# A hybrid decoder kernel: the matrix-memory update taken by pairs of chunks, and the cached values in two halves of TensorE's columns

## The chip, the cores and the metric

The kernel is one program on one core of a Trainium2 chip. The metric is the device time of one execution in microseconds, and for a kernel the median of its runs.

A core has engines that run beside each other and wait for one another through semaphores. The profile calls them PE (TensorE's matmuls), PEld (its weight loads), DVE (VectorE), ACT (ScalarE), POOL (GpSimd) and SP (which here only issues DMAs). A matmul on full fp32 operands has two records in the trace, one for each pass; a transpose, and a product of the large matrices in the kernel's fp32r halves, has one.

## What is computed

A trunk of two layers runs for one prompt of 1024 tokens and eight sample tokens. Each layer has a projection `w_in`, sliding-window attention for eight heads (group A), a matrix memory for eight other heads (group B), an output projection `w_out`, a gated feed-forward and a per-layer embedding. The change concerns group B on the prompt, and the attention of the sample tokens over cached keys and values:

```python
def mlstm_chunk(carry, inp):          # one chunk of 128 tokens, the carry goes to the next
    ...
    sc = jnp.einsum('bhtk,bhsk->bhts', q, k) * dw
    num = iw[..., None] * jnp.einsum('bhvk,bhtk->bhtv', C, q) + jnp.einsum('bhts,bhsv->bhtv', sc, v)
    den = iw * jnp.einsum('bhk,bhtk->bht', n, q) + jnp.sum(sc, axis=-1)
    h = num / jnp.maximum(jnp.abs(den), jnp.exp(-m_t))[..., None]
    ...
    C_new = cw[..., None, None] * C + jnp.einsum('bhs,bhsv,bhsk->bhvk', ws, v, k)
    n_new = cw[..., None] * n + jnp.einsum('bhs,bhsk->bhk', ws, k)
```

```python
def dilated_gather_stats(q, k_all, v_all, window, dilation, buf_len):   # sample tokens, three patterns
    ...
    s = jnp.einsum('bthd,btjhd->bthj', q.astype(jnp.float32), kg) * (HEAD_DIM ** -0.5)
    ...
    o = jnp.einsum('bthj,btjhd->bthd', e, vg) / l[..., None]
```

## The kernel before

The program is written out by hand: every engine has its own list in Python, in the order in which the engine runs it, and waits name a semaphore and a count (`at(...)` adds the layer's offset). Nothing reorders it. A large product is split into a rounded half `hi` and a rest `lo`, so each product of a weight tile is three matmuls (`three`, L923 to L925). GpSimd makes the rest of every weight block (`split`, L868) after ScalarE has rounded it (`round_block`, L1483).

Group B's stage goes over four head pairs, `q` = 0 to 3, and in each over eight chunks `c` of 128 tokens. While TensorE works on pair `q` it also computes the projection of pair `q + 1` in small pieces (`next_products`), five or six steps of three matmuls before each chunk (`ahead_b`). Pair 3 has no next one: there the pieces are the cached values of the sample tokens (`sample_values`, L1038), 24 matmuls of 64 output rows by 512 columns. The stage takes from about 380 to 640 us in layer 0 and from about 1966 to 2221 us in layer 1; the output projection follows it.

For a chunk, TensorE runs, in this order:

- `kq` (L1216): keys by queries for the two heads, each on 64 of the array's 128 rows, into PSUM banks 0 and 1. It waits until the chunk before has been read out.
- the update U (L1271): weighted keys by values, 128x130.
- the chunk's own output (L1290): two matmuls of 65 columns.
- the output from the memory C (L1295), 130 columns, which needs the memory after the chunk before (`c_upd`).

VectorE's part is `prepare(c)`: weighted keys (L2327) and masked scores (L2331); and `finish(c)`: it waits for the update and both outputs, writes the new memory in place (L2341), and makes the output rows (L2345 to L2349), which set `n_read`. Behind them it has the sample tokens' keys: `sample_keys` (L2366, L2367), 24 pieces in pairs 0 and 1, one or two behind each chunk, from two buffers in `kvb`. SP loads piece i when piece i-2 has been used, and every third piece also needs a row of queries. Pair 0 also has a reciprocal square root there.

At the end of a head pair TensorE turns the memory (L1310), which needs the last `finish`; then it goes on with `next_products(0, 6)` and `turn_qk` of the next pair.

In pair 3, VectorE also updates the sample tokens' memory, behind the chunks given: `memory_gates` (1), `memory_keys` (2, waits for `state_C`), `memory_output` (3), `y_sums`, `memory_gated` (waits for `mo_in`, L779's DMA) and `memory_update` (5), then `y_root` and `normalise(0..2)` (6). ScalarE scales and rounds two blocks of `w_out` meanwhile, between the squares of the outputs (`output_squares`, L1689), and GpSimd multiplies the gates in (`gated`, L887), then splits the two blocks one behind the other. After the chunks, TensorE turns the rows of three token tiles (`turn_y`, L1199), ScalarE and VectorE write their halves (L1786, L2438), and the output projection starts; behind its first eighth stands `turn_y(3)`, which needs `y_root(2, ...)` (L2253) and `normalise(3)` (L2265, L2266).

## Time and profile before

| | |
|---|---|
| median of 3 runs | 3222.62 us (3222.48 to 3223.53) |
| span of the profiled execution | 3219.3 us |
| PE busy in it | 3117.2 us, 97% |
| DVE busy | 1854.2 us, 58% |
| mean granted TensorE clock | 0.990 |
| matmul records | 19459 |

The span goes from the first to the last instruction; the median of the runs is 3.3 us above it, which is what lies around the instructions. "Granted clock" is 1.00 at TensorE's upper level, 2.4 GHz, and 0.50 at 1.2 GHz. In rows with a bracket, the bracket is how long the engine had been idle before the row and what it had waited for. The end of a matmul is modelled: a record of 128 columns lasts some 0.27 us, but the next can start 0.11 us after it; so the cost of matmuls is read from the distance of their starts.

### The profile page before, as it was taken

The page shows a single profiled execution, that of the slowest core. Times are in us where ns is not written, and L with a number is a line of the kernel's source. Part 1 is how long each engine was busy: PE and PEld are TensorE (multiplying, and loading weights), DVE is VectorE, ACT ScalarE, POOL GpSimd, SP SyncE. Part 2 cuts the span into 40 slices and gives each one's busy share as a digit, 9 for nine tenths or more (in the row PEclk, how much of TensorE's full clock was granted, in tenths as well). Part 3 has the DMA queues.
Part 4 walks back from the last instruction along what each step waited for, and adds up shares of the span by engine and source line. Part 5 has one row for each costly group of instructions (what it writes and reads, how often), then busy time and mean ns, then how long its engine had stood idle before and what let it go on. Part 6 is the DMA issues. An engine that isn't in the chain of part 4 may idle for free.

```text
span 3219.3 us, 50875 instructions
## 1 busy us (share of the span) xinstructions
PE 3117.2 (97%) x19459; PEld 2847.0 (88%) x19459; DVE 1854.2 (58%) x4369; ACT 1027.8 (32%) x2117; POOL 901.3 (28%) x2061
## 2 busy tenths in 40 slices
PE   7999999899999999999999999998999999999999
PEld 7887777599999999999987777766999999999998
DVE  5676465655555555557467755647555555555663
ACT  4444344533111111115344433455321111111251
POOL 3111122505322324223322210333232333223231
PEclk8999999999999999999999999999999999999999
DMA  5211234512111111110221111336111121111111
GB/s 172 55 47 49 56 83 120 177 51 66 40 53 40 40 66 40 53 40 21 94 69 47 47 50 48 109 106 195 53 40 40 40 66 40 53 40 40 40 37 71
DMA packets 228570, 208.87 MB, mean 65 GB/s; under 512 B 36676, under 2 KB 207620, under 8 KB 226736
## 3 DMA queue, kind: packets, MB, share of 16 engines
q1 hardware_dynamic: 228328, 205.62, 21.1%
q8 instruction: 154, 2.52, 0.3%
q14 instruction: 88, 0.72, 0.1%
HBM read 173.96 MB, written 31.61 MB: 64 GB/s over the span
## 4 chain that ended last, share of the span: by engine, by line
PE 87%; DVE 8%; ACT 2%; issue 1%; POOL 1%; DMA 1%; SPq 0%; DVEq 0%; ACTq 0%
PE ps L923 25%; PE ps L925 24%; PE ps L924 24%; PE ps L1095 2%; PE ps L1066 2%; PE ps L1081 2%; POOL wlo L868 1%; PE ps L1038 1%; PE ps L1216 1%; PE ps L1290 1%; DVE lo L1943 1%; DVE att L2112 1%; DVE att L2101 1%; PE ps L1199 0%; PE ps L1031 0%
## 5 line engine op out<-in xcount | busy, mean ns | idle before, releaser
L868 POOL TENSOR_TENSOR wlo<-raw,whi 128x128 fp32r<-128x128 f32 (+3 forms) x1952 | 857.1, 478 | 1833.4 <-ACT whi L1483 1404.9
L923 PE MATMUL ps<-hi,wlo 128*128 128x344 f32 x2880 | 927.8, 322 | 10.0 <-POOL wlo L868 8.1
L925 PE MATMUL ps<-hi,whi 128*128 128x344 f32 x2880 | 922.3, 320 | 0.0
L924 PE MATMUL ps<-lo,whi 128*128 128x344 f32 x2880 | 921.6, 320 | 0.0
L923 PEld LDWEIGHTS ps<-hi,wlo 128*128 128x128 f32 x2880 | 544.4, 189 | 13.6 <-POOL wlo L868 8.6
L925 PEld LDWEIGHTS ps<-hi,whi 128*128 128x128 f32 x2880 | 543.5, 189 | 0.0
L924 PEld LDWEIGHTS ps<-lo,whi 128*128 128x128 f32 x2880 | 542.9, 188 | 0.6
L923 PE MATMUL ps<-whi,lo 128*128 128x512 f32 (+3 forms) x1056 | 413.4, 391 | 4.8 <-POOL wlo L868 4.3
L925 PE MATMUL ps<-whi,hi 128*128 128x512 f32 (+3 forms) x1056 | 390.3, 370 | 0.0
L924 PE MATMUL ps<-wlo,hi 128*128 128x512 f32 (+3 forms) x1056 | 388.7, 368 | 0.0
L2530 DVE TENSOR_TENSOR X<-X,ps 128x344 f32<-128x344 f32 x528 | 268.0, 511 | 184.7 <-PE ps L925 182.9
L1838 ACT ACTIVATE wb<-wb 128x344 f32<-128x344 f32 x132 | 64.9, 492 | 969.2 <-DVE wb L2517 969.2
L923 PE MATMUL ps<-yhi,wlo 128*128 128x344 f32 x1056 | 340.0, 322 | 0.7 <-DVE X L2530 0.7
L925 PE MATMUL ps<-yhi,whi 128*128 128x344 f32 x1056 | 338.3, 320 | 0.0
L924 PE MATMUL ps<-ylo,whi 128*128 128x344 f32 x1056 | 337.4, 319 | 0.0
L923 PEld LDWEIGHTS ps<-whi,lo 128*128 128x128 f32 (+1 forms) x1056 | 196.7, 186 | 67.1 <-issue 28.2
L925 PEld LDWEIGHTS ps<-whi,hi 128*128 128x128 f32 (+1 forms) x1056 | 196.7, 186 | 26.7
L2509 DVE TENSOR_TENSOR wa<-ps,rstd 128x344 f32<-128x344 f32 x132 | 68.2, 517 | 261.6 <-PE ps L925 261.2
L924 PEld LDWEIGHTS ps<-wlo,hi 128*128 128x128 f32 (+1 forms) x1056 | 197.6, 187 | 20.3
L1483 ACT ACTIVATE whi<-raw 128x2048 fp32r<-128x2048 f32 (+3 forms) x106 | 188.1, 1782 | 44.8 <-DMA raw<-in_w_down 33.7
L923 PEld LDWEIGHTS ps<-yhi,wlo 128*128 128x128 f32 x1056 | 198.7, 188 | 1.8 <-DVE X L2530 1.6
L924 PEld LDWEIGHTS ps<-ylo,whi 128*128 128x128 f32 x1056 | 198.3, 188 | 0.2
(325 smaller groups left out, 3873.6 us busy)
## 6 DMA issues: line engine op xcount, KB each, us to landing
raw<-in_w_up SPq DMA_DIRECT2D x44, 1024.0 KB, 5.1
raw<-in_w_in SPq DMA_DIRECT2D x112, 256.0 KB, 4.4
raw<-in_w_down SPq DMA_DIRECT2D x22, 1024.0 KB, 4.9
kvb<-in_cache_win_k SPq DMA_DIRECT2D x48, 256.0 KB, 3.3
cache<-in_cache_win_v SPq DMA_DIRECT2D x42, 256.0 KB, 3.7
X<-x_scratch SPq DMA_DIRECT2D x4, 2064.0 KB, 11.1
raw<-in_w_out SPq DMA_DIRECT2D x8, 1024.0 KB, 8.5
raw<-in_w_ple_gate SPq DMA_DIRECT2D x8, 1024.0 KB, 5.2
```

The source lines that it names most:

```text
L868: pool.tensor_tensor(out=wlo[:, s, r], in0=raw[:, s, r], in1=whi[:, s, r].bitcast(F32), op=ALU.subtract).then_inc(w_split, 1)
L923: nc.tensor.matmul(out, a_lo, b_hi, start=first, stop=False)
L924: nc.tensor.matmul(out, a_hi, b_lo, start=False, stop=False)
L925: return nc.tensor.matmul(out, a_hi, b_hi, start=False, stop=last)
L1038: nc.tensor.matmul(ps[0:HD, 6, :].rearrange("p (k n) -> p k n", k=4), weight_place(i), value_place(i), start=(i == ORDER[0]), stop=(i == O ...
L1066: mm = nc.tensor.matmul(ps[:, 2 * e + a // 4, 0:(b - a) * P].rearrange("p (t n) -> p t n", n=P), q3[r, qb, :], k3[r, a:b, :], start=True, ...
L1081: mm = nc.tensor.transpose(ps[:, 4 + half, (kb % 4) * P:(kb % 4 + 1) * P], att[:, a:a + P], ident[:, :])
L1095: mm = nc.tensor.matmul(ps[HD * e:HD * e + HD, 6, 0:P], zt[:, p % 2, kb, zc:zc + HD], att[:, a:a + P], start=(kb == 0), stop=(kb == qb))
L1483: do(nc.scalar.activation(whi[:, s, 0:used], raw[:, s, 0:used], ACT.Copy), w_hi, wait=False)
L1838: do(nc.scalar.activation(w, w, ACT.Gelu_apprx_tanh), gelu_done, wait=False)
L2509: do(v.tensor_tensor(out=w[:, 2:CH + 2], in0=ps[:, s % 3, 0:CH], in1=rstd[:, col(c)], op=ALU.mult), gate_read)
L2530: do(v.tensor_tensor(out=x, in0=x, in1=ps[:, 5 + (24 * i + j) % 3, 0:CH], op=ALU.add), dn_read, wait=False)
```

## The change

- **Keys by queries, four chunks together.** `kq` makes eight matmuls for four chunks, which fill banks 0 and 1; it runs twice for a head pair (before the first chunk, and in the second pair of chunks) and no longer eight times.
- **Chunks in pairs `j`.** The updates of two chunks stand together, and so do their four own-output matmuls. The outputs from the memory stay apart, with the second chunk's projection piece between them. VectorE's `prepare` and `outputs_b` take two chunks in one instruction each, where they can.
- **Two memory places.** An update reads one place and writes the other, so `states` need not wait for the chunk's own output from memory. `states`, `prepare` and `outputs_b` replace `prepare` and `finish`, and the sample keys of two chunks now stand behind one another.
- **The memory's turn** (`turn_memory`) stands behind `next_products(0, 6)` of the next pair.
- **Cached values.** Two of the 24 matmuls write to PSUM partitions 0 to 63 and 64 to 127; the two sums are added at the end (`sample_out`, `sample_sum`: one instruction more of 64x512, and a reduction over twice the elements).
- **The queue of SP in pair 3:** `state_C` is loaded ahead of the last five value strips.
- In pair 3, `memory_output` moves up behind the second pair of chunks, `memory_gated` stands behind the third, and `y_sums` and `memory_update` between the states and the outputs of the fourth.

```diff
-VALUES = (6, 9, 11, 13, 15, 17, 19, 20, 20)
+VALUES = (6, 10, 14, 18, 20)
@@ sample_values
-                    for i in ORDER[first:last]:
-                        pe.wait_ge(*at(v_in[value_group(i)], (128, 128, 48, 80)[value_group(i)]))
-                        nc.tensor.matmul(ps[0:HD, 6, :].rearrange("p (k n) -> p k n", k=4), weight_place(i), value_place(i),
-                                         start=(i == ORDER[0]), stop=(i == ORDER[-1])).then_inc(v_used, 1)
+                    for n in range(first, last, 2):
+                        for i in ORDER[n:n + 2]:
+                            pe.wait_ge(*at(v_in[value_group(i)], (128, 128, 48, 80)[value_group(i)]))
+                        for z, i in enumerate(ORDER[n:n + 2]):
+                            nc.tensor.matmul(ps[z * HD:(z + 1) * HD, 6, :].rearrange("p (k n) -> p k n", k=4), weight_place(i), value_place(i),
+                                             start=(n == 0), stop=(n + 2 == 3 * NB)).then_inc(v_used, 1)
@@ TensorE
+                def turn_memory(q):
+                    pe.wait_ge(*at(c_upd, 9 * (q + 1)))
+                    ...
-                    def kq(c):
-                        if c:
-                            pe.wait_ge(*at(sc_done, NT * q + c))
-                        for e in range(2):
+                    def kq(half):
+                        for x in range(4):
+                            c = 4 * half + x
+                            for e in range(2):
...
                         next_products(0, 6)
-                        pe.wait_ge(*at(c_upd, 9 * q))
+                        turn_memory(q - 1)
...
-                    for c in range(NT):
-                        ...
+                    for j in range(NT // 2):
+                        g, c = 4 * q + j, 2 * j
                         next_products(ahead_b(q, c), ahead_b(q, c + 1))
+                        ...
+                        pe.wait_ge(*at(sc_done, g + 1))
+                        if j == 1:
+                            kq(1)
+                        ...
+                        if q + 1 == PAIRS:
+                            sample_values(VALUES[j], VALUES[j + 1])
+                        for x in range(2):
+                            if x:
+                                next_products(ahead_b(q, c + 1), ahead_b(q, c + 2))
+                            pe.wait_ge(*at(c_upd, 9 * q + c + x + 1))
+                            nc.tensor.matmul(ps[:, 3 + j % 2, x * VW:(x + 1) * VW], att[:, 2 * SEQ + (c + x) * P:2 * SEQ + (c + x + 1) * P],
+                                             Cst2[:, 2 * (q % 2) + x, :], start=False, stop=(x == 1)).then_inc(n_ready, 1)
@@ VectorE
+                    def states(j):
+                        dve.wait_ge(*at(u_ready, 4 * q + j + 1))
+                        for x in range(2):
+                            c = 2 * j + x
+                            dve.wait_ge(*at(n_ready, NT * q + c))
+                            ...
-                    for c in range(NT):
+                    for j in range(NT // 2):
...
-                        finish(c)
+                        states(j)
+                        if last and j == 3:
+                            y_sums(0, 6)
+                            memory_update()
+                        if j + 1 < NT // 2:
+                            prepare(j + 1)
+                        outputs_b(j)
...
-                            for i in keys_of(q, c):
-                                sample_keys(i)
+                            for c in (2 * j, 2 * j + 1):
+                                for i in keys_of(q, c):
+                                    sample_keys(i)
...
-                        elif c == 3:
                             memory_output()
-                        elif c == 5:
-                            y_sums(0, 5)
+                        elif j == 2:
                             memory_gated()
-                            memory_update()
```

TensorE in head pair 3 of layer 0, from the turn of the memory. Before, with `kq` (L1216) at each chunk and three and two value strips (L1038) behind the first chunks:

```order
L1038 MATMUL ps<-cache,vectors 64x512 x4
L1216 MATMUL ps<-rstd,kT 128x128 x2
L1271 MATMUL ps<-zt,att 128x130
L1216 MATMUL ps<-rstd,kT 128x128 x2
L1290 MATMUL ps<-zt,att 128x65 x2
L1295 MATMUL ps<-Cst,att 128x130
L1038 MATMUL ps<-cache,vectors 64x512 x3
```

And now (`kq` is L1226, the update L1290, own outputs L1306, outputs from memory L1314, value strips L1042):

```order
L1042 MATMUL ps<-cache,vectors 64x512 x4
L1226 MATMUL ps<-rstd,kT 128x128 x8
L1290 MATMUL ps<-zt,att 128x130 x2
L1306 MATMUL ps<-zt,att 128x65 x4
L1042 MATMUL ps<-cache,vectors 64x512 x4
L1314 MATMUL ps<-Cst,att 128x130 x2
L1290 MATMUL ps<-zt,att 128x130 x2
L1226 MATMUL ps<-rstd,kT 128x128 x8
```

Eight `kq` matmuls stand where two stood, and the value strips have moved ahead of the outputs from memory.

TensorE at the end of head pair 0, before (L1310 is the turn of the memory, L923 to L925 are the next pair's projection):

```order
L932 MATMUL ps<-whi,thin 40x512
L1271 MATMUL ps<-zt,att 128x130
L1290 MATMUL ps<-zt,att 128x65 x2
L1295 MATMUL ps<-Cst,att 128x130
L1310 MATMUL ps<-ident,Cst 64x128 x2
L923 MATMUL ps<-whi,lo 128x512
```

And the turn now (L1211), 18 projection matmuls (L925 to L927) later:

```order
L925 MATMUL ps<-whi,lo 128x512
L926 MATMUL ps<-wlo,hi 128x512
L927 MATMUL ps<-whi,hi 128x512
L1211 MATMUL ps<-ident,Cst 64x128 x2
L1055 MATMUL ps<-ident,zt 128x128 x16
```

The turn stands between the last of these and the turn of the next pair's queries and keys (L1055).

VectorE in head pair 1, behind two chunks, before:

```order
L2341 SCALAR_TENSOR_TENSOR Cst<-Cst,cwb,ps 64x65 x2
L2345 SCALAR_TENSOR_TENSOR den<-ps,em 128x2
L2347 TENSOR_TENSOR den<-ps,den 128x2
L2348 RECIPROCAL den<-den 128x2
L2349 TENSOR_TENSOR yb<-ps,den 128x128
L2327 SCALAR_TENSOR_TENSOR att<-zt,att 128x128
L2331 SCALAR_TENSOR_TENSOR att<-ps,att 128x256
L2366 TENSOR_TENSOR kvb<-kvb 128x512
L2367 TENSOR_REDUCE att<-kvb 128x8
L2366 TENSOR_TENSOR kvb<-kvb 128x512
L2367 TENSOR_REDUCE att<-kvb 128x8
```

And now, for a pair of chunks (states L2351, prepare L2336 and L2340, outputs L2360 to L2364), with the first two of the four key pieces behind it:

```order
L2351 SCALAR_TENSOR_TENSOR Cst<-Cst,cwb,ps 64x65 x4
L2336 SCALAR_TENSOR_TENSOR att<-zt,att 128x128 x2
L2340 SCALAR_TENSOR_TENSOR att<-ps,att 128x2x256
L2360 SCALAR_TENSOR_TENSOR den<-ps,em 128x4
L2362 TENSOR_TENSOR den<-ps,den 128x4
L2363 RECIPROCAL den<-den 128x4
L2364 TENSOR_TENSOR yb<-ps,den 128x256
L2381 TENSOR_TENSOR kvb<-kvb 128x512
L2382 TENSOR_REDUCE att<-kvb 128x8
L2381 TENSOR_TENSOR kvb<-kvb 128x512
L2382 TENSOR_REDUCE att<-kvb 128x8
```

Two more key pieces follow without other work between them, then the next pair's states.

## Rows read from the trace of the kernel before

**Rows 1.** The page: busy time, and the chain that ended last

```profile
PE 3117.2 (97%) x19459; PEld 2847.0 (88%) x19459; DVE 1854.2 (58%) x4369; ACT 1027.8 (32%) x2117; POOL 901.3 (28%) x2061
PE 87%; DVE 8%; ACT 2%; issue 1%; POOL 1%; DMA 1%; SPq 0%; DVEq 0%; ACTq 0%
```

**Rows 2.** Windows, layer 0, in pairs 0 and 3: PE, PEld, DVE, ACT, POOL, clock, DMA

```profile
407.00:445.00 38.00, 38.00 (x208) 29.76 (x208) 29.16 (x90) 19.00 (x51) 16.52 (x34) 1.00 0.21 63
582.00:640.00 58.00, 48.97 (x205) 24.88 (x204) 42.98 (x125) 34.72 (x87) 24.54 (x57) 0.88 0.65 218
```

**Rows 3.** Timeline of PE, a chunk of head pair 1, and the next one's memory output

```profile
483.39 0.38 PE L1271 MATMUL ps<-zt,att 128*128 128x130 f32 x2
483.61 0.56 PE L1290 MATMUL ps<-zt,att 128*128 128x65 f32 x4
484.00 0.44 PE L1295 MATMUL ps<-Cst,att 128*128 128x130 f32 x2
484.37 0.49 PE L1216 MATMUL ps<-rstd,kT 64*128 64x128 f32 x4
484.79 0.50 PE L923 MATMUL ps<-whi,lo 128*128 128x512 f32 x1
485.13 0.40 PE L924 MATMUL ps<-wlo,hi 128*128 128x512 f32 x1
485.37 0.39 PE L925 MATMUL ps<-whi,hi 128*128 128x512 f32 x1
...
489.69 0.44 PE L1295 MATMUL ps<-Cst,att 128*128 128x130 f32 x2
```

**Rows 4.** Timeline of PE: matmuls that share the array, or don't

```profile
1960.89 1.97 PE L1095 MATMUL ps<-att,zt 128*64 128x128 f32 x32
...
588.02 3.65 PE L1038 MATMUL ps<-cache,vectors 128*64 128x512 f32 x8
```

**Rows 5.** Timeline of PE: the memory's turn at the ends of pairs 0 and 1

```profile
445.93 0.41 PE L1310 MATMUL ps<-ident,Cst 128*64 128x128 f32 x2 [0.92 <-DVE Cst L2341]
513.42 0.41 PE L1310 MATMUL ps<-ident,Cst 128*64 128x128 f32 x2 [2.47 <-DVE Cst L2341]
```

**Rows 6.** Timeline of DVE, a chunk of head pair 1

```profile
484.59 0.59 DVE L2341 SCALAR_TENSOR_TENSOR Cst<-Cst,cwb,ps 64x65 f32<-64x65 f32 x2 [0.75 <-PE ps L1295]
...
486.67 0.68 DVE L2366 TENSOR_TENSOR kvb<-kvb 128x512 f32<-128x512 f32 x1
...
488.11 0.69 DVE L2366 TENSOR_TENSOR kvb<-kvb 128x512 f32<-128x512 f32 x1
```

**Rows 7.** DMA issues of the keys: the page, then 455:457 (us to landing)

```profile
kvb<-in_cache_win_k SPq DMA_DIRECT2D x48, 256.0 KB, 3.3
...
kvb<-in_cache_win_k SPq DMA_DIRECT2D x2, 256.0 KB, 9.0
```

**Rows 8.** Timeline, pair 3 of layer 0: what DVE and PE wait for

```profile
610.25 2.29 DVE L2222 TENSOR_TENSOR vectors<-vectors,mz 128x2048 f32<-128x2048 f32 x1 [3.95 <-DMA vectors<-in_state_C]
612.92 0.80 PE L1271 MATMUL ps<-zt,att 128*128 128x130 f32 x2 [4.79 <-DVE att L2327]
```

**Rows 9.** Timeline before the turn of the fourth tile, layers 0 and 1

```profile
637.14 6.70 POOL L868 TENSOR_TENSOR wlo<-raw,whi 128x128 fp32r<-128x128 f32 x16
639.66 4.21 DVE L2253 SCALAR_TENSOR_TENSOR yt<-yrs 128x3 f32<-128x3 f32 x1
644.96 1.09 PE L1199 MATMUL ps<-ident,att 128*128 128x128 f32 x8 [1.11 <-DVE att L2266]
2219.22 6.69 POOL L868 TENSOR_TENSOR wlo<-raw,whi 128x128 fp32r<-128x128 f32 x16
2220.82 5.11 DVE L2253 SCALAR_TENSOR_TENSOR yt<-yrs 128x3 f32<-128x3 f32 x1
2227.03 1.09 PE L1199 MATMUL ps<-ident,att 128*128 128x128 f32 x8 [2.02 <-DVE att L2266]
```

**Rows 10.** Windows: granted clock after the wait at 513.4

```profile
514.00:518.00 4.00, 4.00 (x13) 3.16 (x12) 2.90 (x8) 1.50 (x5) 0.41 (x1) 0.60 0.09 11
```

More of the change, by code:

```diff
@@ L1284, in _ @@
                             sample_turn()
[L1285 removed]
+                        if j >= 2:
                             pe.wait_ge(*at(n_read, g - 1))
[L1287 to L1291 removed]
@@ new lines, in _ @@
+                        for x in range(2):
+                            if x:
[3 more added lines that the diff above has]
+                                             Cst2[:, 2 * (q % 2) + x, :], start=False, stop=(x == 1)).then_inc(n_ready, 1)
```

210 lines of the change are left out of this document (99 added, 111 removed).

## The prediction

> **What bounds the kernel now.** I read the page first. Its busy line has PE at 97% of the span, and the chain that ended last goes over PE for 87% and over DVE for 8% [rows 1]. So a change counts where it takes occupied time from TensorE, and where DVE holds TensorE up. I looked at the stage of the head pairs by windows. In pair 0 PE is busy for the whole 38.00 us, at full clock. In pair 3 it is busy for 48.97 of 58, at a clock of 0.88, with DVE busy for 42.98 [rows 2]: TensorE has too little left to do there, and follows DVE. So there are two kinds of stage. In pairs 0 to 2 each us of TensorE counts as long as DVE keeps up; in pair 3 TensorE's work is almost free, and DVE's order of work and the DMAs that it awaits decide. Next I took the timeline of PE for one chunk, to price its switches of form, then every row of PE with a wait in the stage, and for each wait DVE's timeline in the same stretch, to see what it had been doing. Last came the landings of the keys' DMAs.
>
> The sum is made against the profiled execution: its span of 3219.3 us, to which the median adds 3.3 us that lie around the instructions.
>
> **Keys by queries, 8 visits to 2.** The two passes of the output from memory start at 484.00, and the same width took 0.22 us between 483.39 and 483.61, so they are over at about 484.22. The products run at a distance of 0.23 (485.13 to 485.37, and so for all that follow). Without `kq` the second product would start near 484.45; it starts at 485.13 [rows 3]. The visit costs 0.68 us. Its four records of 128 columns, two beside each other, are two passes of about the width that took 0.11 each: 0.22 to 0.24 us of real streaming. So 0.44 us of each visit is going into the form with 64 rows and coming out of it; the weight load before it and the one behind it don't lie under a running matmul. The streaming stays, six visits of eight go: 6 x 0.44 = 2.6 us for each head pair. Pairs 0 to 2 of two layers are six: -15.8 us. If the second visit of a head pair or the new place of `kq` before the updates keeps part of it, less; the lowest I can see is half, -8. For pair 3 I count nothing, since DVE is late there anyway.
>
> The Trainium skill ("TensorEngine Tiling (Array Packing)", Key Properties) says that a change of the tiling mode drains TensorE. The trace agrees in kind, with 0.44 us a visit; the page gives no figure, and the updates and own outputs, whose grouping changes no form, should by it give nothing. They are counted at nothing in the sum too.
>
> **The turn of the memory, behind 18 products.** Today TensorE reaches it at once and waits 0.92 us at the end of pair 0 and 2.47 at the end of pair 1 [rows 5]; layer 1 repeats both within 0.12 us. Now the turn stands 18 x 0.23 = 4.1 us later, which covers both: 2 x (0.92 + 2.47) = -6.8 us. At the end of pair 2 no products stand between, and the wait stays. After the wait of 2.47 us the clock is 0.60 for the next 4 us [rows 10], some 1.6 us lost. I give this no gain, since the next term makes stalls of nearly that length. The cover is gone if DVE is more than 4 us late at the end of pair 1; the next step says how late.
>
> **Keys, now four behind one another.** In pair 1 a key piece takes DVE 1.44 us (486.67 to 488.11), and everything else of a chunk 2.08 (484.59 to 486.67) [rows 6]. Two chunks come to 4.16, some 3.6 with the outputs' four small instructions once for both; four pieces are 5.8. Together that is 9.4 us, while TensorE needs twice 5.69 less two visits of 0.65, or about 10.1 us (484.00 to 489.69) [rows 3]. By busy time DVE fits. But there are two buffers. The third piece's load starts when the first has been read, 1.4 us into the burst, and lands after 3.3 us [rows 7]: at 4.7 instead of 2.9. The fourth's buffer is free at 2.9, and it lands at 6.2, just as the third is done. The burst is then 7.6 us long instead of 5.8, and DVE's cycle 3.6 + 7.6 = 11.2 us. Today one or two pieces stand behind a chunk, and the other work hides their loads. The next outputs from memory need `states`, which stand behind the burst. TensorE's cycles in pair 1 are near 10.1, 11.1 (with `kq(1)` in it) and 8.3 (the last, which has only the next update and one piece of projection before it needs the memory). It waits 1.1 + 0.1 + 2.9 us, of which the 0.75 us that DVE idles today [rows 6] is to be taken once: about 3.2 us in each layer, +6.4. In pair 0, with one piece a chunk, the cycle fits; I add 0.3 a layer, +0.6. The bounds are nothing (the loads land between instructions) and +10 (each lands in 4.2 us).
>
> **Pair 3.** The value strips now share the array. A group of 8 without a partner takes 3.65 us, 0.46 each with 512 columns; 32 records of 128 columns that do share it take 1.97, which is 0.06 each, so 0.24 for 512 [rows 4]. So TensorE's time for the strips about halves, some 5 us a layer. But it waits there, so this alone counts nothing. What matters is DVE's order. Today DVE waits 3.95 us for `state_C`, and TensorE in turn 4.79 for the weighted keys that stand behind it [rows 8]. `state_C` goes ahead of five strips and lands earlier, so that DVE is up to 3.95 us ahead from there on. The next late transfer is `mo_in`, which doesn't move ahead: `memory_gated` awaits it behind the third pair of chunks, and behind it stand the last two chunks. I estimate 3.5 us earlier at the start of the output projection, in either layer. The extra instruction of `sample_out` (0.7 us, as a key piece's first in [rows 6]) and the wider sum (about 1 us) lie behind the start, where DVE has time.
>
> Then comes the place that decides. `y_root`'s three-column instruction L2253, usually 0.2 us, took 4.21 us in layer 0 and 5.11 in layer 1, and it ended with GpSimd's run of 16 splits, at 643.8 and 2225.9; TensorE waited 1.11 and 2.02 us for what stands behind it [rows 9]. GpSimd's splits come behind its gates, and the last gate behind ScalarE's last squares, which in turn wait for the last outputs. I find that these end hardly 0.5 us earlier than now, as `memory_update` now stands ahead of them. The projection starts 3.5 us sooner, but its fourth tile's turn comes at the old time. Gain 0.6 us in both layers together; the wait of TensorE grows to nearly 5 us, and the clock is then low as in [rows 10], 1.6 us once more than today. +1.0 us.
>
> The Trainium skill ("SBUF — State Buffer", SBUF: two separate sides) has a lock for a port pair that VectorE, with two SBUF inputs, and GpSimd share, for one instruction. By that rule DVE should wait for one split, 0.42 us (6.70 over 16), and be free; the row shows ten of them. The measurement decides for the case that I forecast; the rule speaks for the second one below.
>
> **Sum.** -15.8 - 6.8 + 6.4 + 0.6 + 1.0 = -14.6: a span of 3204.7, and 3208.0 us.
>
> **Rivals.** *A, the forecast, 0.45.* L2253's successor is held to the end of the splits again.
>
> *B, not held, 0.27.* It now has two elements a row for three, and may come at another place of GpSimd's run. Then both layers keep their 3.5 us and lose the waits of 1.11 and 2.02 us: 10.1 less 1.6 for a clock that falls anyway, -8.5 where A has +1.0. That is 3198.5 us. For it speaks that in the rest of the trace DVE is seldom held; against it, two of two.
>
> *C, dearer bursts or cheaper visits, 0.18.* The bursts at their bound (+10 for +7.0), or half of `kq`'s saving kept back (+7.9): 3211 to 3216.
>
> *D, the change gives nothing in its main part, 0.06.* If four pairs of `kq` matmuls still cost 0.68 each, the saving of 15.8 is gone, and 3208 + 15.8 = 3224 us. Against it speaks the run of 32 that share the array at 0.06 us each [rows 4].
>
> *E, slower, 0.04.* The keys' loads: two of them took 9.0 us to landing with weights on the way [rows 7]. Should the burst's loads take that, the third piece starts at 10.4 us and the fourth at 11.9, the burst ends at 13.3, and the cycle is 16.9: 5.7 us more than I have, in three cycles of both layers, +34. 3242 us. It decides from loads of some 5.8 us on, where the cycle is 2.5 us longer, which is 15 in six cycles. Against it: the median of 48 is 3.3.
>
> **How the numbers follow.** A at 3208.0 with half of the bursts' bounds either way is 3204 to 3211; B 3195 to 3201; C to 3216. The range 3196 to 3216 holds A, most of B and C, and leaves out D, E and the lower edge of B. A difference from no change shows from about 0.2%, 6.4 us. Faster is below 3216.2: A, B and nearly all of C, 0.89. D and the rest of C are 0.07; E with a larger D 0.04.
>
> **What the changed profile would show.** `kq` in 16 visits, 48 fewer than the 64 of today, and after each other output from memory products at the regular distance, without the 0.68 us. No wait at the memory's turn in pairs 0 and 1. In pair 1 DVE waits for the keys' DMA in the third piece of each burst, TensorE for `states` at the first output from memory, together 3 us a layer. `memory_keys` without a wait of 3.95 us, `memory_gated` with one for `mo_in`. The start of the output projection 3.5 us sooner against the end of pair 2; and the length of the three-column instruction's successor, 4 us or 0.2, which tells A from B. I would be wrong if the second `kq` of a head pair waited for scores not yet read, if `states`, which now wait for two updates and two outputs, came late by themselves in pairs 0 and 2, or if the turn of the memory waited in its new place.

## The result: slower

The changed kernel takes 3234.4 us (median; 3230.1 to 3237.6), the kernel before 3222.6: a ratio of 1.0037, 95% interval 1.0025 to 1.0049. I had forecast 3208.0, faster, in a range of 3196 to 3216, and had given slower 0.04. Run once more, later, it had 3238.8 beside 3223.8, 1.0046 (1.0031 to 1.0061). Below, kernels are compared by their ratio to the kernel before on the same chip as well as by medians, since the kernel before itself had 3220.9 to 3223.8 on the chips used.

The page of the changed kernel, which answers to [rows 1]:

```profile
span 3230.0 us, 50619 instructions
...
PE 3097.3 (96%) x19459; PEld 2843.7 (88%) x19459; DVE 1840.2 (57%) x4211; ACT 1027.8 (32%) x2117; POOL 893.5 (28%) x2061
...
PE 83%; DVE 9%; ACT 2%; issue 2%; DMA 1%; POOL 1%; SPq 1%; DVEq 0%; ACTq 0%
```

TensorE has 20 us less work, as meant, and yet the span is 10.7 us longer. In the chain, SP's queue, which had 0% before, has 1%, and PE has 83% for 87%. Where the time went shows when the span is cut at TensorE's landmarks (starts of the turn of queries and keys, of the first `kq` of a head pair, and of the eighth tile's turn; us in layer 0, layer 1). "Two edits", "pool" and "split first" are kernels of the experiments below.

| stretch | before | changed | two edits | three edits, pool | and split first |
|---|---|---|---|---|---|
| pair 0: first `kq` to pair 1's turn | 43.4, 43.3 | 43.4, 43.1 | 45.0, 45.0 | 41.3, 41.4 | 41.2, 41.3 |
| pair 1: the same | 52.1, 50.6 | 51.1, 51.8 | 52.2, 51.8 | 49.6, 48.8 | 47.3, 47.2 |
| pair 2's turn to its first `kq` | 17.0, 16.9 | 25.6, 25.3 | 17.3, 17.3 | 17.3, 18.1 | 17.3, 17.3 |
| pair 2 | 45.7, 45.7 | 41.9, 41.9 | 41.9, 41.9 | 41.9, 41.9 | 41.9, 41.9 |
| pair 3's first `kq` to the eighth tile's turn | 72.0, 71.0 | 71.2, 72.5 | 73.2, 70.4 | 67.0, 66.4 | 67.1, 66.9 |

One stretch holds more than the whole loss: behind pair 1, 8.6 and 8.4 us. I had not looked at it. Pair 2, the only one without sample keys, gains 3.8 us. Pairs 0 and 1, where most of the saving was to be, gain next to nothing. A stretch is read from one profile, and it can differ by 3 us between two profiles of one kernel: the second profile of the changed kernel has 46.1 and 44.6 us in pair 0 and 52.2 in both layers in pair 1, but 25.6 and 25.5 behind it. The timeline of PE in the changed kernel, layer 0: four rows with waits in pairs 0 to 2, and the memory's turn (L1211):

```profile
445.23 0.49 PE L1314 MATMUL ps<-Cst,att 128*128 128x130 f32 x2 [3.19 <-DVE Cst L2351]
...
449.72 0.38 PE L1211 MATMUL ps<-ident,Cst 128*64 128x128 f32 x2
...
501.75 0.75 PE L1314 MATMUL ps<-Cst,att 128*128 128x130 f32 x2 [2.03 <-DVE Cst L2351]
...
513.15 0.49 PE L1314 MATMUL ps<-Cst,att 128*128 128x130 f32 x2 [1.30 <-DVE Cst L2351]
...
535.99 0.80 PE L925 MATMUL ps<-whi,lo 128*128 128x512 f32 x1 [6.55 <-ACT zt L1563]
```

The turn of the memory (L1211) no longer waits, against 0.92 us in [rows 5]: as forecast. But the last output from memory (L1314) ahead of it waits 3.19, and the projection of the next pair 6.55 us; in layer 1 the waits are 2.79, 1.19, 2.96 and 6.28.

**The wait of 6.55 us, followed back.** TensorE waits for ScalarE (L1563), which frees a PSUM bank. Its timeline in the changed kernel:

```profile
519.50 0.60 ACT L1602 ACTIVATE rstd<-ps 128x512 f32<-128x512 f32 x1 [0.21 <-PE ps L1055]
534.95 0.47 ACT L1559 ACTIVATE zt<-ps,rcol 128x256 f32<-128x256 f32 x1 [14.85 <-DMA z_scratch<-zt]
```

The timeline of SP's queue in the changed kernel:

```profile
511.15 9.41 SPq L669 DMA_DIRECT2D kvb<-in_cache_win_k  x3
520.93 1.15 SPq L741 DMA_DIRECT2D mg<-g_scratch  x2
...
525.96 1.21 SPq L572 DMA_DIRECT2D raw<-in_w_out  x2
527.22 1.25 SPq L638 DMA_DIRECT2D z_scratch<-zt  x2
```

And in the kernel before, in the same place:

```profile
505.84 5.55 SPq L668 DMA_DIRECT2D kvb<-in_cache_win_k  x3
511.76 1.15 SPq L740 DMA_DIRECT2D mg<-g_scratch  x2
...
518.38 1.47 SPq L637 DMA_DIRECT2D z_scratch<-zt  x2
```

ScalarE waits until the sample tokens' rows of pair 2 have been copied out of the place that it is to write. That copy (L638, before L637) stands in SP's queue behind the key loads of pair 1, and a key load waits until a buffer has been used. The last of them went out at 511.4 (505.84 + 5.55) and now at 520.6 (511.15 + 9.41); eight small loads and two weight blocks follow, so the copy is issued at 527.2, not 518.4. VectorE's timeline of the kernel before, from the key whose buffer the last load takes:

```profile
510.35 0.69 DVE L2367 TENSOR_REDUCE att<-kvb 128x8 f32<-128x512 f32 x1
...
515.16 0.22 DVE L2357 COPY cT<-ps 64x64 f32<-64x64 f32 x1
...
515.66 0.69 DVE L2366 TENSOR_TENSOR kvb<-kvb 128x512 f32<-128x512 f32 x1
```

VectorE's timeline of the changed kernel says why that key is used so late:

```profile
511.78 0.69 DVE L2382 TENSOR_REDUCE att<-kvb 128x8 f32<-128x512 f32 x1
512.50 1.24 DVE L2351 SCALAR_TENSOR_TENSOR Cst<-Cst,cwb,ps 64x65 f32<-64x65 f32 x4
...
518.29 0.22 DVE L2372 COPY cT<-ps 64x64 f32<-64x64 f32 x1 [2.64 <-PE ps L1211]
...
519.52 0.69 DVE L2382 TENSOR_REDUCE att<-kvb 128x8 f32<-128x512 f32 x1
520.24 0.69 DVE L2381 TENSOR_TENSOR kvb<-kvb 128x512 f32<-128x512 f32 x1
...
522.97 0.69 DVE L2381 TENSOR_TENSOR kvb<-kvb 128x512 f32<-128x512 f32 x1 [1.32 <-DMA kvb<-in_cache_win_k]
```

Three keys stand behind the copy of the turned memory (L2372) where one stood before. The first of them, whose buffer the last load takes, is done at 520.2 (519.52 + 0.69) and was done at 511.0 (510.35 + 0.69): 9.2 us later, as is the load. Of these, 2.64 us are VectorE's wait for the turn, which has been put 18 products later. The rest comes from the pairing: that key now stands behind the states and outputs of the last two chunks, and stood ahead of the last chunk's.

### The profile page after: what moved, and what is told of

It reads as the page before. It is cut to its first block, busy times and chain, and to the rows that moved or that the text cites. A ratio compares the mean times of both kernels' runs of the same rounds, so it can differ in the third digit from the quotient of the medians.

```text
span 3230.0 us, 50619 instructions
## 1 busy us (share of the span) xinstructions
PE 3097.3 (96%) x19459; PEld 2843.7 (88%) x19459; DVE 1840.2 (57%) x4211; ACT 1027.8 (32%) x2117; POOL 893.5 (28%) x2061
## 4 chain that ended last, share of the span: by engine, by line
PE 83%; DVE 9%; ACT 2%; issue 2%; DMA 1%; POOL 1%; SPq 1%; DVEq 0%; ACTq 0%
PE ps L925 24%; PE ps L927 24%; PE ps L926 24%; PE ps L1099 2%; PE ps L1070 2%; PE ps L1085 2%; POOL wlo L870 1%; DMA kvb<-in_cache_win_k 1%; DVE kvb L2381 1%; DVE lo L1952 1%; PE ps L1306 1%; PE ps L1203 1%; DVE att L2121 1%; DVE att L2382 1%; DVE att L2110 1%
## 5 line engine op out<-in xcount | busy, mean ns | idle before, releaser
L925 PE MATMUL ps<-hi,wlo 128*128 128x344 f32 x2880 | 928.3, 322 | 12.0 <-POOL wlo L870 8.1
L927 PE MATMUL ps<-hi,whi 128*128 128x344 f32 x2880 | 922.5, 320 | 0.0
L925 PEld LDWEIGHTS ps<-hi,wlo 128*128 128x128 f32 x2880 | 544.7, 189 | 15.6 <-POOL wlo L870 8.6
L927 PEld LDWEIGHTS ps<-hi,whi 128*128 128x128 f32 x2880 | 543.8, 189 | 0.0
L925 PE MATMUL ps<-whi,lo 128*128 128x512 f32 (+3 forms) x1056 | 415.1, 393 | 15.4 <-ACT zt L1563 13.2
L927 PE MATMUL ps<-whi,hi 128*128 128x512 f32 (+3 forms) x1056 | 391.3, 371 | 0.0
L925 PE MATMUL ps<-yhi,wlo 128*128 128x344 f32 x1056 | 339.9, 322 | 0.7 <-DVE X L2546 0.7
L927 PE MATMUL ps<-yhi,whi 128*128 128x344 f32 x1056 | 338.3, 320 | 0.0
L925 PEld LDWEIGHTS ps<-whi,lo 128*128 128x128 f32 (+1 forms) x1056 | 198.2, 188 | 74.8 <-issue 27.0
L927 PEld LDWEIGHTS ps<-whi,hi 128*128 128x128 f32 (+1 forms) x1056 | 197.6, 187 | 27.0
L925 PEld LDWEIGHTS ps<-yhi,wlo 128*128 128x128 f32 x1056 | 198.7, 188 | 1.5 <-DVE X L2546 1.3
## 6 DMA issues: line engine op xcount, KB each, us to landing
X<-x_scratch SPq DMA_DIRECT2D x4, 2064.0 KB, 10.7
```

What stands on the lines that cost most here:

```text
L925: nc.tensor.matmul(out, a_lo, b_hi, start=first, stop=False)
L927: return nc.tensor.matmul(out, a_hi, b_hi, start=False, stop=last)
```

## The experiments

**Small loads last.** In SP's queue of pair 1 the small loads go behind the copies.

```diff
-                    if h2 == 1:
-                        ...
                     if p < 2 * PAIRS - 2:
                         load_pair(p + 3)
                     store_pair(p + 1)
                     sp.wait_ge(*at(o_exp, h2 + 1))
                     sp.dma_start(Zd[6, :, h2 * P:h2 * P + P], zt[0:NB, p % 2, NT, OG:ZW]).then_inc(z_stored[p % 2], 16)
+                    if h2 == 1:
+                        ...
```

> The changed kernel, but in SP's queue of head pair 1 the twelve small loads for the memory of the sample tokens (gates, m, n) stand behind the copy of the third pair's sample rows and not ahead of it. Queue theory: TensorE's new wait of 6.55 and 6.28 us at the start of pair 2 is the end of a chain: the last key piece is used late, SP's queue can't pass its load, and the copy that ScalarE awaits stands behind it and behind 5.0 us of small issues. Then the copy goes 5.0 us sooner, the wait falls to about 1.5 us in each layer and the clock stays up: some 12 to 14 us less than the changed kernel's 3234.4, so 3221 to 3223. Rival, key bursts alone: the 8.5 us lost there come from DVE being late behind the keys; the order of small loads does nothing, 3232 to 3236, wait as before.

(There are eight of these loads, not twelve.) 3229.8 us, 1.0024 (1.0014 to 1.0035). TensorE's waits are 2.00 and 1.31 us, the stretch takes 19.5 and 18.8. So the small loads have a part in the wait, as said, but the median is only 5 us lower, where the stretch gave up 12.6: in this profile pair 3 takes 74.0 and 74.7 us to the eighth tile's turn.

**Keys before the turned memory.** In pair 1 `store_turned` goes behind the last keys.

```diff
                             if j == 3:
                                 tile_sum(p + 1)
-                                store_turned()
+                                if q != 1:
+                                    store_turned()
                             ...
                                     sample_keys(i)
+                            if j == 3 and q == 1:
+                                store_turned()
```

> The changed kernel, but at the end of head pair 1 VectorE takes the last four key pieces ahead of the copy of the turned memory, for which it waited 2.6 us in the new place. Queue theory: the last key load is released about 3.4 us sooner, so the copy lands 3.4 us sooner and TensorE waits about 3.1 us and not 6.5: 3227 to 3229. If the moved turn has no part in it: no change, 3232 to 3236. A cost of its own: TensorE may wait for the turned memory's bank, up to 1 us.

3228.7 us, 1.0017 (1.0006 to 1.0028); the waits are 2.70 and 2.18 us. The time is as expected and the waits are a little shorter. So the keys' place behind the turn's copy has a part.

**The turn at the end of its pair**, the other way round.

```diff
-                        turn_memory(q - 1)
...
                                              Cst2[:, 2 * (q % 2) + x, :], start=False, stop=(x == 1)).then_inc(n_ready, 1)
+                    turn_memory(q)
```

> The changed kernel, but the memory's turn stands at the end of its head pair, as before. The prediction's term said that moving it behind 18 products saves 6.8 us: undone, 3234.4 + 7 = 3241. Queue theory: states now stand ahead of the outputs, so the turn waits under 1 us there, and the copy of the turned memory, and with it the last keys and the rows' copy, come 3.5 us sooner: 3228 to 3231.

3233.5 us, 1.0040 (1.0025 to 1.0055): neither theory's time. The waits behind pair 1 fall to 2.84 and 1.23 us and that stretch to 21.9 and 18.8, as the queue theory has it, but the median is only 0.9 us under the first runs of the changed kernel, and the interval holds the ratios of both of its measurements, 1.0037 and 1.0046. It is not 7 us higher either. In its timeline of PE the turn at the end of pair 1 does not wait:

```profile
515.73 0.80 PE L1313 MATMUL ps<-Cst,att 128*128 128x130 f32 x2 [2.96 <-DVE Cst L2350]
516.37 0.64 PE L1211 MATMUL ps<-ident,Cst 128*64 128x128 f32 x2
```

So the turn had nothing to gain from the move, since `states` now come ahead of the outputs. Where the 10 us of the stretch went is open: its profile has them spread over pairs 0, 1 and 3, by amounts that also differ between profiles of one kernel.

**Both order edits**, beside the changed kernel itself on one chip.

> The changed kernel once more, unchanged, beside the next one. It had 3234.4 us (3230.1 to 3237.6), ratio 1.0037. Expected again 1.003 to 1.0045; it shows how far kernels with idle stretches of TensorE differ from one chip and profile to the next.

> The changed kernel with the small loads behind the rows' copy and the last keys ahead of the turned memory's copy, and the bursts of keys as they are. Queue theory: the wait of 6.55 and 6.28 us at the start of pair 2 is gone in both layers and the stretch from the turn of pair 2's queries to its first key-query products takes 17 us instead of 25.5: up to 17 us, of which pair 3 may take back 2 to 5 (as with the small loads last): 12 to 15 us less than the changed kernel beside it, so 3220, about the kernel before. If the queue is not the cause of most of it: 5 to 8 us.

The changed kernel again: 3238.8 us, 1.0046 (1.0031 to 1.0061). With both edits: 3221.6 us, 0.9994 (0.9985 to 1.0004), 17.2 us less, more than the 12 to 15 expected and as much as the stretch behind pair 1 gives up (8.3 and 8.2 us: 25.6 and 25.5 to 17.3). TensorE has no wait there:

```profile
521.60:538.90 17.30, 17.30 (x90) 12.56 (x89) 6.86 (x14) 8.83 (x29) 0.00 (x0) 1.00 0.60 181
```

In the changed kernel the same window (columns as in [rows 2]) is:

```profile
518.00:543.60 25.60, 19.05 (x91) 13.48 (x89) 8.92 (x16) 9.81 (x32) 0.00 (x0) 0.87 0.50 140
```

19.05 us of work instead of 17.3 at a clock of 0.87, and 6.55 of wait. This settles the cause of the loss: the copy that comes late in SP's queue. What is left, no gain, has to come from pairs 0 and 1.

**Keys around the outputs.** Two of a burst's keys go ahead of `outputs_b`, which waits for TensorE anyway.

```diff
+                        early = [i for c in (2 * j, 2 * j + 1) for i in keys_of(q, c)]
+                        early = early[:2] if len(early) > 2 and j < 3 else []
+                        for i in early:
+                            sample_keys(i)
                         outputs_b(j)
...
-                                    sample_keys(i)
+                                    if i not in early:
+                                        sample_keys(i)
```

> The changed kernel, but where more than two key pieces follow in one burst, the first two stand ahead of the outputs (j below 3), so that DVE works on them while it would wait for TensorE's second output from memory, and the third piece's load has the outputs' 1 us and that wait to land. Burst theory: TensorE's waits for the states inside pairs 0 and 1 (2.79 to 3.19, 1.2 to 2.0, 1.3 to 3.0 us, 13.5 us in the two layers) shrink to a third, and with the queue wait untouched the time falls by 7 to 9 us: 3225 to 3227. Rival: these waits come from two pairs of chunks' states being taken together, not from the bursts: under 2 us.

3223.7 us, 1.0001 (0.9992 to 1.0011): 10.7 us less than the changed kernel, more than the 7 to 9 expected. Inside pairs 0 and 1 six waits of 13.5 us became one of 0.98 and three for the projection's next piece of 1.38, 1.14 and 1.57, and pair 1 takes 47.2 and 47.4 us. The queue's wait is still 6.59 and 6.31. This shows that the waits come from the bursts; they cost 13.5 us where I had 7.0. In the changed kernel a burst of pair 1 looks like this:

```profile
479.48 0.69 DVE L2381 TENSOR_TENSOR kvb<-kvb 128x512 f32<-128x512 f32 x1
...
480.92 0.69 DVE L2381 TENSOR_TENSOR kvb<-kvb 128x512 f32<-128x512 f32 x1
...
483.57 0.69 DVE L2381 TENSOR_TENSOR kvb<-kvb 128x512 f32<-128x512 f32 x1 [1.24 <-DMA kvb<-in_cache_win_k]
...
486.60 0.69 DVE L2381 TENSOR_TENSOR kvb<-kvb 128x512 f32<-128x512 f32 x1 [1.62 <-DMA kvb<-in_cache_win_k]
...
488.05 1.23 DVE L2351 SCALAR_TENSOR_TENSOR Cst<-Cst,cwb,ps 64x65 f32<-64x65 f32 x4
```

8.6 us from the first key to the states, where I had 7.6; the other bursts of pair 1 have DMA waits of 3.41 and 1.40 us. And in pair 0 a burst of three at 436.5 waits 3.48 us for its third, a burst that I had priced at 0.3.

**The kernel before, with `kq` in fours** in pairs 0 and 1 only.

```diff
+                        if q < 2 and c % 4:
+                            return
+                        for x in range(4 if q < 2 else 1):
                             for e in range(2):
-                                mm = nc.tensor.matmul(ps[:, e, 0:P], kT[r, c * P:(c + 1) * P], ...
+                                mm = nc.tensor.matmul(ps[:, e, x * P:(x + 1) * P], kT[r, (c + x) * P:(c + x + 1) * P], ...
```

> The kernel before, with only one part of the change: in head pairs 0 and 1 the key-query products of four chunks are made together (two visits for eight), everything else where it was; pairs 2 and 3 as before. Drain theory (0.44 us saved a visit, six visits in each of four head pairs of the two layers): -10.6 us, 3212. Rival: the drain is paid again elsewhere, or DVE, which takes 42% longer to get a free chunk, holds TensorE at the end of each pair, so the wait at the memory's turn grows and half of it is lost: 3217. If nothing is saved: 3222.6.

3223.1 us, 1.0006 (0.9995 to 1.0017): nothing. (The 42% in the expectation had no basis and stands for nothing.) Its timeline of PE in pair 1:

```profile
474.13 0.38 PE L1274 MATMUL ps<-zt,att 128*128 128x130 f32 x2
...
479.17 0.38 PE L1274 MATMUL ps<-zt,att 128*128 128x130 f32 x2
...
489.28 0.38 PE L1274 MATMUL ps<-zt,att 128*128 128x130 f32 x2
...
490.27 1.16 PE L1219 MATMUL ps<-rstd,kT 64*128 64x128 f32 x16
...
495.66 0.39 PE L1274 MATMUL ps<-zt,att 128*128 128x130 f32 x2
...
509.80 0.49 PE L1274 MATMUL ps<-zt,att 128*128 128x130 f32 x2 [0.63 <-DVE att L2330]
...
514.53 0.64 PE L1313 MATMUL ps<-ident,Cst 128*64 128x128 f32 x2 [3.46 <-DVE Cst L2345]
```

A chunk without a visit takes 5.04 us, one with the visit of four 6.38, against 5.69 each in [rows 3]: 4 x 5.69 - 3 x 5.04 - 6.38 = 1.26 us for four chunks, 2.5 a head pair. My 2.6 was right. But the pair as a whole is no shorter: the turn's wait grew from 2.47 to 3.46 us, with 0.63 more ahead of it, and in pair 0 three waits of 0.37, 0.80 and 1.02 stand for the one of 0.92. VectorE, which in pair 1 of layer 0 waited 6.8 us for outputs from memory (L1295) before, waits 3.5 us for them here, and 2.0 for keys. So it has little slack in pairs 0 and 1: time taken from TensorE there comes back as waits for VectorE, and those at the pairs' ends were the sign of it. The granted clock has a part too, 0.94 in pair 1 in both layers for 0.97 and 1.00.

**The kernel before, with the values in halves.**

```diff
-VALUES = (6, 9, 11, 13, 15, 17, 19, 20, 20)
+VALUES = (6, 8, 10, 12, 14, 16, 18, 20, 20)
...
-                                         start=(i == ORDER[0]), stop=(i == ORDER[-1])).then_inc(v_used, 1)
+                                             start=(n == 0), stop=(n + 2 == 3 * NB)).then_inc(v_used, 1)
```

> The kernel before, with only the values part: two of the 24 matmuls share the array and write to 64 partitions each, six ahead, then two behind each chunk; one more instruction of 64x512 and a reduction twice as wide. Theory of the prediction: 5 us of TensorE's work less in pair 3 of each layer is worth nothing there, as DVE decides; within 1 us of 3222.6. Rival: less work means more idle time and a lower granted clock in pair 3 (0.87 and 0.91 before, 0.78 in the changed kernel), which lengthens what follows: 1 to 4 us slower.

3220.9 us, 0.9999 (0.9989 to 1.0008): no difference, as predicted. The clock in pair 3 fell (0.68 from its first `kq` to the first tile's turn in layer 0, for 0.87), and the time does not show it; TensorE waits there in both kernels.

**Three edits.** Small loads last, keys before the turned memory, keys around the outputs.

> The changed kernel with three edits of order together: the small loads behind the sample rows' copy, the last keys of pair 1 ahead of the turned memory's copy, and two of each burst's keys ahead of the outputs. Queue theory: each alone left a part of the wait at the start of pair 2 (1.3 to 2.0 us with the small loads last, 2.2 to 2.7 with the keys first); together it is gone, and that stretch takes 17.0 us again instead of 25.5; the two layers give 17 us, of the kernel with the keys around the outputs at 3223.7: 3205 to 3209. Rival, from the traces of the last kernels: pair 3 takes what is gained before it (38.6 us to the first turned tile instead of 36.1 in layer 0), since a transfer there lands at a fixed time: 3213 to 3217.

3212.3 us, 0.9972 (0.9962 to 0.9982). Between the two theories; the stretch behind pair 1 is 17.4 and 17.3 us, but pair 1 takes 49.5 and 49.7, as TensorE now waits 2.23 and 2.55 us for GpSimd's splits at its end.

**Three edits, and GpSimd's last 16 splits wait for the root.**

```diff
                         gated(q, NT - 1, NT)
+                        pool.wait_ge(*at(yr_two, 1))
                         split(B + n + 1)
```

> The kernel with three edits, and GpSimd's last run of 16 splits waits until VectorE has the root for the last two tiles. Hold theory: the root's first instruction took 5.99 and 6.27 us only because it met the run of splits; now it takes 0.2, the fourth tile's turn comes 5 us sooner in each layer, TensorE's waits of 2.9 and 3.2 us go, with some of the low clock behind them: 5 to 8 us less than the three edits alone. Rival: the instruction waits for something else that comes at that time (an activation, a square), then it keeps its 6 us; or the splits, now 1.5 us later, hold TensorE in the projection: no gain.

3202.5 us, 0.9937 (0.9921 to 0.9954): 9.8 us less than without it, more than expected. From the first tile's turn to the eighth it takes 30.7 and 30.9 us, for 35.0 and 35.4. This is the place where A and B parted. In the changed kernel the root's first instruction for two tiles was held longer than in [rows 9], again to the end of GpSimd's run (646.7):

```profile
640.78 5.99 DVE L2262 SCALAR_TENSOR_TENSOR yt<-yrs 128x2 f32<-128x2 f32 x1
...
640.05 6.69 POOL L870 TENSOR_TENSOR wlo<-raw,whi 128x128 fp32r<-128x128 f32 x16
```

and with the splits waiting for it:

```profile
631.53 0.15 DVE L2263 SCALAR_TENSOR_TENSOR yt<-yrs 128x2 f32<-128x2 f32 x1
...
632.16 7.08 POOL L870 TENSOR_TENSOR wlo<-raw,whi 128x128 fp32r<-128x128 f32 x16 [1.65 <-DVE yrs L2265]
```

**The same wait alone**, in the changed kernel and in the kernel before.

> The changed kernel with the wait of GpSimd's last 16 splits for the root alone. With the three edits it was worth 9.75 us. The hold was 5.99 and 6.27 us here: 8 to 10 us less than the changed kernel, 3224 to 3227. If the gain of 9.75 needed the other edits (which move the stage against the transfers), under 4 us.

> The kernel before, with only the wait of GpSimd's last 16 splits for the root. Its instruction L2253 was held 4.21 and 5.11 us and TensorE waited 1.11 and 2.02 us behind it, so the kernel before has the cost too, but less of it: 3 to 5 us, with the low clock behind the waits, 3217 to 3219. If before and changed kernel gain alike (9 us), the hold has no part in the change being slower.

Changed kernel with it: 3230.5 us, 1.0036 (1.0023 to 1.0049), not the 8 to 10 us less that were expected. Against the changed kernel's first runs it is 3.9 us less by medians and nothing by the ratio, against the second ones (1.0046) 3 us by the ratio, inside both intervals, although in its profile the root takes 0.16 us and the tiles' stretch 30.1 and 30.0 us for 35.1 and 36.1. The same profile has 2.6 us more in pair 0 of layer 0 and 3.6 more between the layers; the first is no effect of the wait, since the changed kernel's second profile has it without (46.1). That the place gains is shown; how much of it the time keeps is open. The kernel before with it: 3217.4 us, 0.9989 (0.9980 to 0.9999), 3 to 4 us, as expected. Both kernels gain about alike, so no part of the changed kernel's loss is shown to come from the hold.

**The root by columns**, with the splits as they were (and "split first", below).

```diff
+                    if n == 2:
+                        for x in range(end - first):
+                            y1, t1, s1 = y[:, x:x + 1], t[:, x:x + 1], s[:, x:x + 1]
+                            do(v.tensor_scalar(t1, y1, y1, -0.5 / WA, ALU.mult, ALU.mult))
+                            do(v.tensor_scalar(t1, s1, WA * EPS, t1, ALU.add, ALU.mult))
+                            do(v.tensor_scalar(y1, t1, 1.5, y1, ALU.add, ALU.mult))
+                        return
```

> The kernel with three edits and the first splits ahead of the gates, without the wait in GpSimd's queue; the root of the last two tiles is made column by column with instructions that read one tensor from SBUF (and a column as their scalar), six of 0.16 us for three. If the hold comes from the instruction's second tensor input: no hold, 3197 to 3201, as with the wait in GpSimd's queue (3199.6). If any instruction at this place is held by the run of splits: the first of the six takes 6 us, 3208 to 3211.

3203.5 us, 0.9938 (0.9923 to 0.9952), the ratio of the kernel with the wait. Both theories were half right. VectorE, behind four more of the six:

```profile
628.43 0.22 DVE L2269 TENSOR_SCALAR yt<-ssq,yt 128x1 f32<-128x1 f32 x1
628.68 0.21 DVE L2270 TENSOR_SCALAR yrs<-yt,yrs 128x1 f32<-128x1 f32 x1
628.93 4.95 DVE L2284 TENSOR_SCALAR att<-att,yrs 128x384 f32<-128x384 f32 x1
```

None of the six is held, though GpSimd's run goes from 626.95 to 633.66. The next instruction, a multiplication over 384 columns from SBUF to SBUF, is. In this profile pair 3 takes 70.9 and 69.6 us to the eighth tile's turn, longer than with the wait (67.1 and 66.9 in the next kernel but one), and the stretch between the layers is 4.4 us shorter than there; so the ratio alone does not show that the columns are as good as the wait.

**Key-query products in twos**, in the best kernel so far.

```diff
-                    def kq(half):
-                        for x in range(4):
+                    def kq(j):
+                        for x in range(2):
...
-                        if j == 1:
-                            kq(1)
+                        if j < 3:
+                            kq(j + 1)
```

> The kernel with three edits and the wait in GpSimd's queue (3202.5), but the key-query products are made for two chunks at a time: four visits for each head pair, not two. Each visit costs TensorE 0.41 to 0.44 us beside its streaming, and TensorE now hardly waits in pairs 0 to 2: 2 visits x 6 head pairs x 0.42 = 5 us more, 3207.6. If TensorE's time is given back in the waits there, as in the kernel before with key-query products in fours (0.2 us of the 10.6 expected), no change.

3206.0 us, 0.9958 (0.9944 to 0.9973): 3.5 us more by medians, as expected in sign and near in size (5), though the two intervals overlap. Where TensorE hardly waits, a visit does cost about what I said.

**The first splits ahead of the gates** in pairs 0 and 1.

```diff
-                        gated(q, 0, 2)
+                        if q == 2:
+                            gated(q, 0, 2)
                         split(B + n)
+                        if q < 2:
+                            gated(q, 0, 2)
```

> The kernel with three edits and the wait in GpSimd's queue (3202.5), and in head pairs 0 and 1 GpSimd splits the first of its two weight blocks ahead of the first two gates, not behind. TensorE now waits 2.50 and 2.27 us for a split at the end of pair 1, and 1.2 us at the end of pair 0 of layer 1. The block is rounded long before the gates' inputs are there, so the splits come 8 us sooner and these waits go, with the low clock behind two of them: 6 to 9 us less, 3194 to 3197. If VectorE, which shares the time with GpSimd, becomes slower by the overlap or the waits pass to its states: 3200 to 3203.

3199.6 us, 0.9936 (0.9920 to 0.9953). The waits for splits at the end of pair 1 are 1.45 and 1.43 us, for 2.50 and 2.27; they were to go whole. Pair 1 takes 47.3 and 47.2 us, 2.3 and 1.6 less. The median is 2.9 us less, where 6 to 9 were expected, and the ratio is the same, so the gain is not settled by the timing. It is the lowest median of all kernels, 21 us under the kernel before on the same chip (3220.9) and 18 us under the kernel before with the wait in GpSimd's queue.

## Why the prediction was wrong

**The steps that failed** are the turn of the memory and the keys, in what they left out. Of the turn I said "18 x 0.23 = 4.1 us later, which covers both": I looked at who waits for it on TensorE, and not at what stands behind it on VectorE, three keys. The step on the keys priced a late burst by TensorE's next output from memory, and did not follow a late key into SP's queue, where a copy that ScalarE awaits, and TensorE after it, stands behind its load and ten other issues. In pair 1 of layer 0 the last load went out 9.2 us later, and TensorE waited 6.55 us. The 17 us that the stretch behind pair 1 lost stand in none of my terms and rivals; E, the slower one, had the loads themselves slow. Two edits of order take the wait away, and 17.2 us came back with it. That the turn alone, put back, takes most of the wait away is shown; that it gives time back is not.

**Keys by queries, -15.8.** The size of a visit was right: 1.26 us for four chunks, where I had 1.3. What was wrong is where it counts. The text said "each us of TensorE counts as long as DVE keeps up", and took from VectorE's busy time that it does. The waits at the pairs' ends [rows 5] already showed that there it doesn't; I booked their removal as a second gain. In the kernel before the term alone, in pairs 0 and 1, is worth nothing. My three terms come to -10.3 us for pairs 0 and 1 of both layers (-10.5 of the -15.8, -6.8, +7.0), and the table has 0.0 (5.7 more in the second profile): without its waits TensorE takes 7 us less there, and its waits are 7 us longer. In pair 2, with no keys, the whole was 3.8 us a layer where I had 2.6; the turn's wait of 0.77 us at its end, which I had left untouched, went too.

**The turn, -6.8.** Its waits did go, and came back one matmul earlier, at the output from memory. The 18 products were not what removed them: with the turn back at the end of its pair it does not wait in pairs 0 and 1 either.

**The bursts, +7.0.** Right in kind, the third and the fourth piece wait for their loads; the term was half of what was measured, 13.5 us, which also lies outside its bound of 10. A burst took 8.6 us and not 7.6, and pair 0, which I had at 0.3 us a layer, had 3.19 and 2.79. (By its own numbers the step gives 3.35 us a layer in pair 1, not 3.2.)

**Pair 3, +1.0.** From its first `kq` to the eighth tile's turn, 71.2 and 72.5 us for 72.0 and 71.0: +0.8. `memory_keys` had no wait and `memory_gated` 2.95 us for `mo_in`, as said. Rows of VectorE's and TensorE's timelines in the changed kernel, layer 0:

```profile
613.14 2.29 DVE L2231 TENSOR_TENSOR vectors<-vectors,mz 128x2048 f32<-128x2048 f32 x1
...
625.29 0.46 DVE L2244 TENSOR_TENSOR mh<-mh,mz 128x32 f32<-128x32 f32 x1 [2.95 <-DMA mz<-z_scratch]
...
640.96 0.39 PE L925 MATMUL ps<-hi,wlo 128*128 128x344 f32 x1 [1.11 <-issue]
...
647.87 1.31 PE L1203 MATMUL ps<-ident,att 128*128 128x128 f32 x8 [2.89 <-DVE att L2275]
```

The successor of L2253 was held again, 5.99 and 6.27 us: case A, right in kind. The size was in part luck. The output projection started 2.4 and 1.0 us sooner against the turn of pair 3's queries (L925, layers 0 and 1), where I had 3.5 in either, and TensorE waited 2.89 and 3.17 us for the fourth tile, where I had nearly 5: the two misses offset each other, because the fourth tile's turn came at the old time, as said.

## What to carry to other kernels

A step that is moved takes along what stands behind it on every engine; follow those instructions to the buffers that they free, and from there into the DMA queue, to the first transfer that someone else awaits. A wait at the end of a stage is a sign of who sets the stage's length, which busy shares don't tell; here, time taken from the waiting engine came back as longer waits. Put work that frees a buffer ahead of an instruction that would wait anyway. Here five small shifts of order, of which the last is not shown to add anything, turned a change that cost 12 us into one that gives 20; one of the five, the wait in GpSimd's queue, gives 3 to 4 us in the kernel before too.

## What the runs showed of the hardware

**VectorE held to the end of a run of GpSimd.** The Trainium skill ("SBUF — State Buffer", Who interferes with whom) has VectorE's instructions with two inputs from SBUF, and the two-port modes that `tensor_scalar` can enter, contend with GpSimd, each for the length of one instruction. The trace agrees on who: the two-input instruction was held and, when it was gone, the wide `TENSOR_SCALAR`, though no run shows which mode that was in; six of one column between them were not. On how long, it does not contradict the page in pair 1, where in the kernel before the key products that are longer than 0.69 us, all beside splits, take 0.76 to 0.99: a wait of less than one split (0.42). But behind the third tile's turn the hold lasted 4 to 7 us, up to sixteen splits, in both layers of all 12 profiles in which that run has not been made to wait. And it is not that place alone: in 9 of the 17 profiles an instruction between the layers, where no kernel here differs, has it too, as with the first splits ahead of the gates:

```profile
1638.95 6.04 DVE L2007 TENSOR_TENSOR rowr<-zt 128x768 f32<-128x768 f32 x1
```

In the other 8 it takes 0.96 us or a little more. The stretch between the layers took 1291.8 to 1295.6 us in the nine and 1290.2 to 1291.2 in seven of the eight (1294.4 in one), so the hold goes with a longer stretch. Whether it makes executions of one kernel differ is not shown: both profiles of the changed kernel are without it. What starts such a hold is open.

**The form with 64 rows** costs TensorE 0.65 us a visit taken out of a chunk of pair 1 (5.69 - 5.04). The visit of four takes 1.34 (6.38 - 5.04), so streaming is 0.23 a visit ((1.34 - 0.65) / 3), and some 0.42 us is for going in and out. No run here separates the change of form from the weight loads around it.
